# Experts' weights in twelve places instead of six, and token picks and weighted rows made per pair of experts inside the loop

## What is computed

```python
weights = g_p[:, None] * top_p                       # two experts of one group per token
expert_id = (g_sel[:, None] * EXPERTS_PER_GROUP + top_i).astype(jnp.int32)
flat_tok = jnp.repeat(jnp.arange(N, dtype=jnp.int32), TOP_K_IN_GROUP)
y = grouped_expert_ffn(xt, expert_id.reshape(-1), flat_tok, weights.reshape(-1), w_gate, w_up, w_down)
```

## Time and profile before

| | us |
|---|---|
| median of 3 runs | 2373.82 (2372.65 to 2374.21) |
| the profiled execution | 2373.23 |
| its span | 2371.4 |
| TensorE busy | 2263.5 (95%) |
| VectorE busy | 1209.8 (51%) |
| ScalarE busy | 911.4 (38%) |
| DMA, last fifth of the span | 404 to 416 GB/s, elsewhere 105 to 255 |

### The profile page before, as it was taken

How to read it: one execution, slowest core, us unless ns; L and a number is a source line. 1 busy time by engine, 2 the same in 40 slices (tenths; PEclk the granted TensorE clock), 3 DMA queues, 4 the chain that set the end, 5 groups by cost and what they waited for, 6 DMA issues and landing times.

```text
span 2371.4 us, 36570 instructions
## 1 busy us (share of the span) xinstructions
PE 2263.5 (95%) x15002; PEld 1860.3 (78%) x15002; DVE 1209.8 (51%) x2087; ACT 911.4 (38%) x1101; POOL 30.8 (1%) x61
## 2 busy tenths in 40 slices
PE   7999999998999999999999899999978899999997
PEld 7998868898999989887788899998757544555553
DVE  4786765387676268868545777862243100000001
ACT  5455423464655155563235546542222211111111
POOL 0000000000000000000000000000000000000000
PEclk9999999999999999999999999999988999999998
DMA  6464333534455555643334354555443599999995
GB/s 255 171 210 169 105 115 113 184 134 163 175 178 194 179 185 184 209 152 114 107 126 176 125 180 175 179 196 216 163 157 125 213 404 410 415 411 412 412 410 222
DMA packets 70755, 499.38 MB, mean 211 GB/s; under 512 B 8304, under 2 KB 8304, under 8 KB 11744
## 3 DMA queue, kind: packets, MB, share of 16 engines
q1 hardware_dynamic: 66096, 481.65, 53.9%
q0 software_dynamic: 4384, 14.77, 1.9%
q10 hardware_dynamic: 144, 1.05, 0.1%
HBM read 496.29 MB, written 1.15 MB: 210 GB/s over the span
## 4 chain that ended last, share of the span: by engine, by line
PE 86%; DVE 7%; ACT 5%; issue 1%; DMA 0%; DVEq 0%; ACTq 0%
PE bank L840 22%; PE bank L850 12%; PE bank L845 11%; PE bank L1264 9%; PE bank L1290 5%; PE bank L1052 3%; PE bank L1246 3%; PE bank L1304 3%; PE bank L984 3%; PE bank L785 2%; PE bank L797 2%; PE bank L1275 1%; PE bank L828 1%; PE bank L1167 1%; DVE ring_r L2168 1%
## 5 line engine op out<-in xcount | busy, mean ns | idle before, releaser
L850 PE MATMUL bank<-u,ring 128*128 128x256 f32 x1152 | 255.0, 380 | 0.0
L850 PEld LDWEIGHTS bank<-u,ring 128*128 128x128 f32 x1152 | 217.9, 191 | 29.5 <-issue 0.8
L2483 DVE COPY arena<-bank 128x256 f32<-128x256 f32 x32 | 13.6, 425 | 445.3 <-PE bank L1275 445.3
L2168 DVE TENSOR_TENSOR ring_r<-ring,weights_and_u_split 128x2048 fp32r<-128x2048 f32 x80 | 183.2, 2292 | 74.4 <-ACT weights_and_u_split L1626 70.7
L840 PE MATMUL bank<-weights_and_u_split,hidden_and_weights_high 128*128 128x256 f32 x1600 | 202.1, 284 | 0.0
L840 PEld LDWEIGHTS bank<-weights_and_u_split,hidden_and_weights_high 128*128 128x128 f32 x1600 | 195.4, 192 | 4.7 <-issue 4.3
L845 PE MATMUL bank<-weights_and_u_split,ring_r 128*128 128x256 f32 x1496 | 196.4, 283 | 0.0
L845 PEld LDWEIGHTS bank<-weights_and_u_split,ring_r 128*128 128x128 f32 x1496 | 187.0, 192 | 0.0
L1626 ACT ACTIVATE weights_and_u_split<-ring 128x2048 fp32r<-128x2048 f32 x80 | 152.5, 1909 | 81.0 <-PE bank L845 40.1
L1455 ACT ACTIVATE arena<-bank 128x512 f32<-128x512 f32 x96 | 57.0, 594 | 295.8 <-PE bank L850 186.7
L2168 DVE TENSOR_TENSOR ring_r<-ring,hidden_and_weights_high 128x2048 fp32r<-128x2048 f32 x60 | 137.2, 2288 | 32.0 <-ACT hidden_and_weights_high L1626 32.0
(11 more groups left out here) (394 smaller groups left out, 3727.3 us busy)
## 6 DMA issues: line engine op xcount, KB each, us to landing
ring<-stream SPq DMA_DIRECT2D x393, 1024.0 KB, 4.9
arena<-stream SPq DMA_DIRECT2D x64, 1024.0 KB, 10.4
arena<-rows_scratch POOLq DMA_DIRECT2D x48, 256.0 KB, 4.0
con<-con_d SPq DMA_DIRECT2D x1, 1344.5 KB, 9.5
h<-x_d ACTq DMA_DIRECT2D x1, 1024.0 KB, 9.7
out<-arena SPq DMA_DIRECT2D x1, 1024.0 KB, 3.9
arena<-con_d POOLq DMA_DIRECT2D x1, 864.0 KB, 7.2
par<-par_d POOLq DMA_DIRECT2D x2, 422.0 KB, 6.2
```

The source lines that it names most:

```text
L850: mm = pe.matmul(bank[:, c * S:(c + 1) * S], w[:, k, c * P:(c + 1) * P], x[:, k, :], start=(k == 0), stop=(k == KC - 1))
L2168: tt(ring_r[:, POS[k] % RING, :], w, high(k).bitcast(F32), ALU.subtract).then_inc(wlo_ok.sem, 1)
```

## The change

1. Twelve places for the experts' weights: eight in `arena`, four in the ring. Five units are issued early, between the ring's loads of the second block's input projection, each behind the same `h_new` wait; the next seven as places come free, the last when the router has run. SyncE's ring loop ends at the first block's end; the rest of its loads are written out one by one. From then on unit m is issued when unit m-12 has been used. Six semaphores of the first block are taken over for six of the places, with the value that they had there as base (`E_BASE`).
2. `pick` and `pickw` are made for one pair of experts at a time, by instructions of 128x256, in VectorE's loop (`pair_picks`, `pair_weights`); two before the branch's first gather, the others a pair ahead.
3. The block of `ws` products and ScalarE's 16 copies are gone. The same eight records per expert follow inside `slot_turn`, into the other half of the PSUM bank that it writes, and VectorE copies the working place straight from PSUM.
4. `dense()` is changed too (its weight row is spread per expert); it doesn't run here, but its code is shorter.

```diff
-ERING = 6
+ERING = 12
+E_EARLY = 5
...
+        E_AT = {n: 64 + 8 * n for n in range(E_EARLY)} | {n: 24 + 8 * (n - 8) for n in range(8, 11)}
...
+        e_landed += [one.sem for one in (lb_in, lb_exp, nega_exp, sp_abs, sp_ln, rows_ok)]
+        E_BASE = [0] * (ERING // 2) + [DEPTH] * (ERING // 2)
...
-            with sp.Fori(1, total // RING) as i:
+            looped = min(total, B2) // RING
+            with sp.Fori(1, looped) as i:
...
-            for n in range(total // RING * RING, total):
+            for n in range(looped * RING, total):
                 sp.wait_ge(unit_done.sem, n - RING + 1)
                 sp.dma_start(ring[:, n % RING, :], stream[n]).then_inc(landed[n % RING], 16)
+                early = n - B2 - WIN2 - 3
+                if second and 0 <= early < E_EARLY:
+                    sp.wait_ge(h_new.sem, h_new.at(DEPTH, 0))
+                    sp.dma_start(e_slot(early), stream[B2 + MOE + early]).then_inc(e_landed[early], 16)
             if second:
-                sp.wait_ge(h_new.sem, h_new.at(DEPTH, 0))
-                for n in range(ERING):
-                    if n >= ERING - RING:
-                        sp.wait_ge(unit_done.sem, B2 + MOE + n - ERING + 1)
+                for n in range(E_EARLY, ERING):
+                    free = n - E_EARLY + WOUT2 + 1 if n < 8 else ROUTER - 1 if n < 11 else ROUTER
+                    sp.wait_ge(unit_done.sem, B2 + free + 1)
                     sp.dma_start(e_slot(n), stream[B2 + MOE + n]).then_inc(e_landed[n], 16)
-                with sp.Fori(1, EXPERTS) as i:
+                with sp.Fori(1, EXPERTS * 6 // ERING) as i:
...
-            def slot_turn(r, c):
-
+            def slot_turn(i, c):
+
+                r = i * 2
                 pe.wait_ge(hs_ok, r + (c + 1))
+                pe.wait_ge(pkw_ok, i + (c // 2 + 1))
                 if c or not isinstance(r, int):
-                    pe.wait_ge(ht_cp, r + c)
+                    pe.wait_ge(wn_cp, r + c)
                 for k in range(4):
...
+                for k in range(T):
+                    for g in range(2):
+                        mm = pe.matmul(A[4][g * 64:(g + 1) * 64, S + k * P:S + (k + 1) * P], pickw[:, k, c % 2, :], ident,
+                                       start=True, stop=True)
                 mm.then_inc(ht_mm, 1)
...
             def compact():
-                pe.wait_ge(pick_ok, 1)
...
-                pe.wait_ge(pickw_ok, 1)
-                for q in range(PAIRS):
-                    if q >= 4:
-                        pe.wait_ge(ws_cp, q - 3)
...
-                for q in range(PAIRS):
-                    act.wait_ge(ws_mm, q + 1)
-                    act.activation(flat(WS + 2 * q, 2), A[q % 4][:, :], ACT.Copy).then_inc(ws_cp, 1)
...
-                V.tensor_copy(arena[:, WNOW[c % 2], :], ws[:, r + c, :]).then_inc(wn_cp, 1)
+                V.tensor_copy(arena[:, WNOW[c % 2], :], A[4][:, S:2 * S]).then_inc(wn_cp, 1)
...
+            def pair_picks(q):
...
+                if not isinstance(q, int) or q:
+                    dve.wait_ge(x_mm, q * 2)
+                    dve.wait_ge(pkw_ok, q)
+                tt(pick, at, iota, ALU.is_equal).then_inc(pick_ok, 1)
...
+            def pair_weights(q):
...
+                dve.wait_ge(pick_ok, q + 1)
+                if not isinstance(q, int) or q:
+                    dve.wait_ge(ht_mm, q * 2)
+                tt(pickw, pick, w, ALU.mult).then_inc(pkw_ok, 1)
...
                 with dve.Fori(0, PAIRS - 2) as i:
+                    pair_weights(i + 1)
+                    pair_picks(i + 2)
                     for a in range(2):
```

More of the change, by code:

```diff
@@ L388, in program @@
         landed = [sem(f"weights_landed{i}") for i in range(RING)]
-        e_landed = [sem(f"expert_weights_landed{i}") for i in range(ERING)]
+        e_landed = [sem(f"expert_weights_landed{i}") for i in range(ERING // 2)]
         par_in, con_in, x_in, stored = sem("par_landed"), sem("constants_landed"), sem("x_landed"), sem("stored")
@@ L508, in e_slot @@
             n = m % ERING
-            if n < ERING - RING:
-                return flat(MORE_SLOTS + 8 * n, 8)
-            return ring[:, (B2 + MOE + n - (ERING - RING)) % RING, :]
+            if n in E_AT:
+                return flat(E_AT[n], 8)
+            return ring[:, (B2 + MOE + (n - E_EARLY if n < 8 else RING - 1)) % RING, :]
         def use2(m):
@@ L653, in program @@
         utok = flat(UTOK, 8).rearrange("p (i n) -> p i n", i=T)
[L654 to L657, removed]
+        pick, pickw = (flat(at, 1).rearrange("p (i e s) -> p i e s", i=T, e=2) for at in (PK, PKW))
+        pick2 = flat(PK, 1).rearrange("p (i n) -> p i n", i=T)
         xe = flat(XE, 4).rearrange("p (c n) -> p c n", c=KC)
@@ L664, in program @@
         block = ctx.enter_context(nc.Block())
-        assert 6 == ERING
+        assert 12 == ERING and B2 % RING == 0
         @block.sync
@@ L1213, in _, with spread_row @@
             mm.then_inc(r_cum, 1)
+            def spread_row(e):
+                pe.wait_ge(wb_free, e + 1)
+                pe.wait_ge(r_wT, e + 2)
+                pe.matmul(A[4][:, 0:S], ones[0:32, :], arena[0:32, ROW, :], start=True, stop=True).then_inc(wb_mm, 1)
             def dense():
@@ L1221, in dense @@
                 mm.then_inc(r_T, 1)
-                pe.wait_ge(r_wT, 1)
-                for q in range(EXPERTS // 2):
-                    if q >= 4:
[L1226 to L1232, removed]
+                spread_row(0)
                 moe_units((0, 4), 1, (0, 0), True)
+                spread_row(1)
                 with pe.Fori(0, (EXPERTS - 2) // 2) as i:
                     for a in range(2):
-                        moe_units((i * 2 + a, 10), i * 2 + (a + 2), (i * 2 + (a + 1), (a + 1) % 2), False)
+                        moe_units((i, 10 + 6 * a), i * 2 + (a + 2), (i * 2 + (a + 1), (a + 1) % 2), False)
+                        spread_row(i * 2 + (a + 2))
                 moe_units((0, UNITS2 - MOE - 2), None, (EXPERTS - 1, 1), False)
             def pick_tokens(q, n):
+                if not n:
+                    pe.wait_ge(pick_ok, q + 1)
                 if n or not isinstance(q, int) or q:
@@ L1314, in compact @@
                 slot_gate_up(0, 1)
-                pe.wait_ge(pickw_ok, 1)
-                for q in range(PAIRS):
-                    if q >= 4:
-                        pe.wait_ge(ws_cp, q - 3)
-                    for a in range(2):
-                        for i in range(T):
-                            for g in range(2):
-                                mm = pe.matmul(A[q % 4][g * 64:(g + 1) * 64, a * S + i * P:a * S + (i + 1) * P],
-                                               pickw[:, i, 2 * q + a, :], ident, start=True, stop=True)
-                    mm.then_inc(ws_mm, 1)
                 slot_turn(0, 0)
@@ L1355, in moe_units @@
             def moe_units(first, e_gate, e_down, start):
-                six, rest = first
+                pair, rest = first
                 n = 0
@@ L1366, in moe_units @@
                     at = rest + n
-                    pe.wait_ge(e_landed[at % ERING], (six + (at // ERING + 1)) * 16)
+                    pe.wait_ge(e_landed[at % ERING], pair * 16 + (16 * (at // ERING + 1) + E_BASE[at % ERING]))
                     w = e_slot(at).rearrange("p (k m) -> p k m", k=2)
```

91 lines of the change are left out of this document (46 added, 45 removed).

## The result

| | before | changed |
|---|---|---|
| median, same chip (us) | 2374.02 (2372.31 to 2376.78, 6 runs) | 2384.03 (2381.81 to 2386.62, 6 runs) |
| profiled execution (us) | 2373.23 | 2385.07 |
| its span (us) | 2371.4 | 2383.2 |
| mean clock of TensorE, share of full | 0.979 | 0.977 |

The change makes the kernel slower by 0.41%: the ratio is 1.0041, 95% interval 1.0030 to 1.0052. The prediction was 2379.5 us, within 2372.0 to 2384.5. Direction and range held, but the loss is 10.0 us where 5.7 were forecast.

What follows compares the result with a forecast made beforehand. TensorE was taken to bound the kernel, not the transfers. 2373.23 - 14.1 (block) + 21.3 (loop and its ends) - 1.3 (start) = 2379.1 us, stated as 2379.5; range 2372.0 to 2384.5.

Steps and rivals of the forecast that it cites:

- The bound: In the experts' loop TensorE sets the pace, busy 30.64 of 30.64 us a pass; the transfers just keep up.
- Rival C: In the experts' stage the transfers are the bound after all: 15.3 us saved besides the picks' 1.3, 2357 us; chance 0.04.
- Places: 0: Six more places for experts' weights bring 15.3 us of transfer before the stage, hidden under TensorE: worth 0.
- Rival E: Early expert loads delay the second block's input projection by up to 12.7 us: 2392 us; chance 0.05.
- The records: -14.1 and +14.1: The block before the experts' loop goes, -14.1 us; the same records in the experts' turns cost +14.1 us.
- Changes of form, +4.8, and lost overlap, +2.4: In the turns: 0.15 us per expert for another tile form, +4.8 us; turn and sum no longer overlapping, +2.4 us.
- Rival B: In the turns the moved records cost only 55.1 ns each and overlap stays: 2372.5 us; chance 0.12.
- VectorE, 0: VectorE's added work in the loop, about 0.9 us a pass, stays covered: 0; uncovered, up to 12.6 us.
- The branch as what is late next, -1.65: Before the first gather, picks by pair gain only 1.65 us, since TensorE's own 3.77 us branch is late next.
- Rival D: The longer loop's code isn't all held, so back jumps cost 3.56 us each: +46 us, 2426 us; chance 0.05.
- The clock, +0.3 on balance: At the first gathers, one group more or less at half clock is 1.73 us either way; +0.3 us taken.
- The start as a whole: From picks by pair to the first gathers, branch and clock included: -1.3 us, from -3.4 to +0.1.

Runs made afterwards that it cites:

- b_first_pick: The kernel before with only the first pair's picks made in an instruction of their own, ahead of the rest: 2375.02 us, ratio 1.0003.

## Why the prediction was right, and where its size was off

- **The bound.** TensorE, not the transfers. Right: six places and twelve give the same pass, and without the products the pass is 30.64 us again. Rival C is out.
- **Places: 0.** Right, by the same runs. Rival E is out: the projection's stages shift by the 2.02 us of the program's start and no more. The prediction named a move of the stages before 1834 us as a sign of being wrong; they moved, but the move is there at 30 us and comes also with the code of the kernel before (`b_first_pick`).
- **The records: -14.1 and +14.1.** Right. With the products beside gate/up the pass grows by 0.87 us, twice the 0.44 of eight records.
- **Changes of form, +4.8, and lost overlap, +2.4.** Right in mechanism and size: 7.2 forecast, 7.30 in the profile, and 7.2 vanish when the same products stand beside their like. The pass was forecast at 31.96 and is 31.96; the turn to the next at 1.6 and is 1.62; turn and sum at 3.5 and are 3.55. That the 0.15 us of a change of form came out to the hundredth has some luck in it: it was a choice between 0.10 and 0.22. Rival B is out as an account of the change, but its figure is what the better place reaches.
- **VectorE, 0.** Right, by the run without the products.
- **The branch as what is late next, -1.65.** Right: -1.52 measured, behind a branch of 3.85 us for 3.77. The run with `compact()` directly behind the branch, 92 ns, shows that the 3.8 us are the jump's. The Trainium skill (Runtime: NRT & Kernel Launch, Instruction fetch mechanics) says that a taken branch whose target isn't in the code held must fetch it first. The traces agree: one packet of code during each of the 3.77, 3.85 and 3.59 us, none during the 92 ns.
- **Rival D**, the loop's code out of reach: out. The loop's jumps take 76 to 247 ns, and from 1930 to 2330 us only the weights' queue has packets.
- **The clock, +0.3 on balance.** This is the term that was mis-sized, and with it the sum. The prediction saw that a sooner start need not bring a sooner rise and priced one group more or less at half clock at 1.73 us; taking the middle of "either way" it booked 0.3. Measured: +3.45, twice the price of one group. The start as a whole, booked at -1.3 with ends of -3.4 and +0.1, came to +1.93, beyond its upper end. The clock rose 6.9 us later: the whole second gather and the first 3.6 us of gate/up ran at half. The run that starts late again takes this back (1.94 us sooner at expert 1's gate/up, which is 3.45 less its own later start of 1.55, to 0.04 us). The run with the likely side behind the branch shows that a start some 2 us sooner still had the clock's early rise again: neither sign nor size could be read off the rows before.

The terms so come to 2373.8 + 7.3 + 1.9 = 2383.0, one us below the median of 2384.03. Of the 4.5 us by which the forecast was low, 3.2 are the start; the last us isn't explained and is of the size of the scatter of medians.

## What to carry over

Before more buffers or earlier loads are bought, compare the rate at which an engine can use the data with the rate at which it comes: where a pass is one engine's busy time, only its instructions count. A small product that is moved belongs beside products of its own tile form, and not between two that overlap on different rows; where it stands was worth 7 of 10 us here, more than anything else in this change. A start moved forward while the clock is at half is to be costed with the clock's rise later as well as sooner; here 1.5 us sooner cost time, and 4.0 us sooner gained it. And look at the branch ahead of it: put the side that is taken right behind it.

## What the runs showed of the hardware

- A change between matmul tile forms (64*128 and 128*64) costs 0.10 to 0.22 us in these loops (0.15 where one more was put in), though the engine shows as busy all along: it shows in the distance of starts, not in busy time.
- TensorE's branch over the other side's code takes 3.3 to 3.9 us in ten kernels, with one packet of code fetched meanwhile in each; falling through it takes 88 to 95 ns in three. The profile books it as "issue" or hides it under another engine's wait; only the sequencer's own line shows it.
- Starting 1.5 us sooner made the clock rise 6.9 us later, 20.5 us at half in place of 13.7; starting sooner still (5.5 us after the fall in place of 7.7) gave 13.7 again. In 3 of 11 runs of one kernel the times are about 5 us lower and the mean clock higher, as without the late rise. Nothing here tells what decides this.
- Idle products kept the clock at full through the gap, but each group held up the work queued behind it, and 1.6 us were left of the gain.
